# Attention scores of both query tiles of a head issued together, every second step, in a two-layer hybrid encoder

## What is computed

```python
# differential attention: 8 heads, two maps per head (m = 0, 1), head width 64, queries in blocks of 128
logits = jnp.einsum("bqhmd,bkhmd->bhmqk", q_blk, k) * scale
p = jax.nn.softmax(logits + bias[None, :, None], axis=-1)
attn = p[:, :, 0] - lam * p[:, :, 1]
out = jnp.einsum("bhqk,bkhe->bqhe", attn, v)
# beside it, independent of it: a bidirectional Mamba-2 scan (32 heads in 4 groups, 2 chunks of 128 tokens)
lmat = jnp.exp(segsum(a));  cb = C @ B.T;  y_diag = (cb * lmat) @ X;  y_off = C @ state * exp(a_cum)
```

## Time and profile before

| | us |
|---|---|
| device time, median of three runs | 1744.72 |
| lowest and highest of the three | 1743.62, 1745.13 |
| span of the profiled execution, first to last instruction | 1742.8 |
| PE busy | 1694.6 (97% of the span) |
| DVE, ACT, POOL busy | 713.3, 685.1, 668.0 |
| span of the attention and scan loop, each layer (from 198 to 303 in layer 0) | about 105 |

### The profile page before, as it was taken

One profiled execution on the slowest core, in us unless ns is written; L12 is line 12 of the kernel. 1 busy time (PEld: TensorE's weight loads), 2 busy tenths in 40 slices (PEclk: granted clock), 3 DMA queues, 4 the chain that ended last, 5 costly groups with the idle time before them and its releaser, 6 DMA issues.

```text
span 1742.8 us, 23270 instructions
## 1 busy us (share of the span) xinstructions
PE 1694.6 (97%) x8975; PEld 1056.7 (61%) x8975; DVE 713.3 (41%) x1345; ACT 685.1 (39%) x1549; POOL 668.0 (38%) x536
## 2 busy tenths in 40 slices
PE   8999999999999999899999999999999999999997
PEld 6889877787434444343378898777864344443343
DVE  5728788524212212121276387865241212222122
ACT  5565787754211111111156567877541111111111
POOL 7888876894000000000077887768930000000000
PEclk9999999999999999999999999999999999999999
DMA  7554312667999999999954442227589999999997
GB/s 271 195 193 152 140 49 108 274 259 308 363 415 427 428 427 428 427 428 428 411 229 165 179 189 97 97 80 300 219 333 398 420 427 427 428 427 428 428 425 303
DMA packets 50707, 528.47 MB, mean 303 GB/s; under 512 B 5496, under 2 KB 8312, under 8 KB 20128
## 3 DMA queue, kind: packets, MB, share of 16 engines
q1 hardware_dynamic: 50560, 526.89, 74.2%
q0 software_dynamic: 32, 0.02, 0.0%
HBM read 525.82 MB, written 1.06 MB: 302 GB/s over the span
## 4 chain that ended last, share of the span: by engine, by line
PE 68%; DMA 9%; DVE 9%; SPq 5%; ACT 5%; issue 2%; POOL 1%; DVEq 0%; ACTq 0%
PE PS L1297 19%; PE PS L1325 10%; DMA view<-in_w_exp_down_dram 9%; PE PS L875 8%; PE PS L877 8%; PE PS L876 8%; SPq L678 5%; DVE view L2003 5%; PE PS L1237 2%; PE PS L1223 1%; DVE view L1999 1%; PE PS L1082 1%; PE PS L1224 1%; PE PS L863 1%; ACT view L1571 1%
## 5 line engine op out<-in xcount | busy, mean ns | idle before, releaser
L2370 POOL TENSOR_TENSOR view<-view,view 128x512 fp32r<-128x512 f32 x448 | 579.8, 1315 | 548.1 <-ACT view L1457 537.3
L1297 PE MATMUL PS<-view,view 128*64 128x512 f32 x2044 | 457.8, 600 | 15.1 <-issue 14.5
L1457 ACT ACTIVATE view<-view 128x512 fp32r<-128x512 f32 x448 | 275.1, 633 | 149.1 <-PE PS L877 146.9
L1297 PEld LDWEIGHTS PS<-view,view 128*64 128x64 f32 x2044 | 150.9, 138 | 292.0 <-issue 288.7
L875 PE MATMUL PS<-view,view 128*128 128x512 f32 x704 | 286.0, 406 | 5.6 <-POOL view L2370 3.7
L877 PE MATMUL PS<-view,view 128*128 128x512 f32 x704 | 275.5, 391 | 0.0
L876 PE MATMUL PS<-view,view 128*128 128x512 f32 x704 | 275.4, 391 | 0.0
L1325 PE MATMUL PS<-view,stb 128*64 128x512 f32 x1024 | 230.4, 597 | 8.4 <-DMA view<-in_w_exp_down_dram 5.5
L2270 DVE SCALAR_TENSOR_TENSOR view<-PS,gcol,view 128x512 fp32r<-128x512 f32 x64 | 48.1, 751 | 448.7 <-ACT view L1770 448.6
L875 PEld LDWEIGHTS PS<-view,view 128*128 128x128 f32 x704 | 132.8, 189 | 33.5 <-issue 5.8
L1325 PEld LDWEIGHTS PS<-view,stb 128*64 128x64 f32 x1024 | 71.3, 136 | 132.6 <-issue 117.0
(11 more groups left out here) (260 smaller groups left out, 2024.0 us busy)
## 6 DMA issues: line engine op xcount, KB each, us to landing
view<-in_w_exp_up_dram SPq DMA_DIRECT2D x56, 2048.0 KB, 25.8
view<-in_w_exp_down_dram SPq DMA_DIRECT2D x56, 2048.0 KB, 28.1
view<-in_w_mix_dram SPq DMA_DIRECT2D x54, 2048.0 KB, 7.7
view<-in_w_exp_gate_dram SPq DMA_DIRECT2D x52, 2048.0 KB, 28.8
view<-in_w_exp_gate_dram SPq DMA_DIRECT2D x20, 512.0 KB, 31.2
view<-in_w_exp_down_dram SPq DMA_DIRECT2D x20, 512.0 KB, 14.9
view<-in_w_exp_gate_dram SPq DMA_DIRECT2D x8, 1024.0 KB, 8.1
view<-in_w_exp_up_dram SPq DMA_DIRECT2D x8, 1024.0 KB, 9.3
```

The source lines that it names most:

```text
L1297: ins = pe.matmul(bank(ph, name, j)[e * CAP:(e + 1) * CAP, :], xgT1[:, k, at + e * CAP:at + (e + 1) * CAP], rows, start=(k == 0), stop=(k ...
L1457: nc.scalar.activation(highs(chunk), weights(slot8, chunk), ACT.Copy).then_inc(*high_ready.up(ph))
L2370: g_.tensor_tensor(weights(low8, chunk), weights(slot8, chunk), highs(chunk), ALU.subtract).then_inc(*low_ready.up(ph))
```

## The change

`scores` is called once for each head, in the even step, and issues the products of both query tiles: those of the second tile go to columns 256 to 511 of the same two banks. There is one fill and one drain of the pair of banks for each head, where there were two. DVE reads columns 0 to 255 in the even step and 256 to 511 in the odd step; the even step's read counts on DVE's own step semaphore, and the odd step's read counts the drain. The number of matmuls, of DVE instructions and of bytes is the same.

```diff
@@ mixer_fills
-            f += [(("D", j, q), 4), (("sc", i), 6)]
+            f += [(("D", j, q), 4)] + ([(("sc", j), 6)] if q == 0 else [])
@@ SP
-                        sp.wait_ge(*out_of(ph, "sc", ATT - 1))
+                        sp.wait_ge(*out_of(ph, "sc", HEADS - 1))
@@ PE
-                def scores(i):
-                    h, qt = i // 2, i % 2
-                    pe.wait_ge(*free(ph, "sc", i))
-                    if i == 0:
+                def scores(h):
+                    pe.wait_ge(*free(ph, "sc", h))
+                    if h == 0:
                         pe.wait_ge(*out_of(ph, "xT", XT))
-                    for m in range(2):
-                        rows = slice(m * HD, (m + 1) * HD)
-                        ins = pe.matmul(PS[:, 6 + m, 0:TT * P], qT[rows, h, qt * P:(qt + 1) * P], kT[rows, h, :],
-                                        start=True, stop=True)
-                    ins.then_inc(*fill(ph, "sc", i))
+                    for qt in range(TT):
+                        for m in range(2):
+                            rows = slice(m * HD, (m + 1) * HD)
+                            ins = pe.matmul(PS[:, 6 + m, qt * TT * P:(qt + 1) * TT * P], qT[rows, h, qt * P:(qt + 1) * P],
+                                            kT[rows, h, :], start=True, stop=True)
+                    ins.then_inc(*fill(ph, "sc", h))
@@ PE, step i
                             decay_sums(i)
-                            scores(i)
+                            if q == 0:
+                                scores(j)
@@ DVE, step i
-                        dve.wait_ge(*full(ph, "sc", i))
+                        dve.wait_ge(*full(ph, "sc", h))
...
-                        v.scalar_tensor_tensor(out=lg[:, i % 2], in0=PS[:, 6:8, 0:TT * P],
-                                               scalar=HD ** -0.5, in1=bias, op0=ALU.mult, op1=ALU.add
-                                               ).then_inc(*drain(ph, "sc", i))
-                        dve.wait_ge(*out_of(ph, "sc", i))
+                        ins = v.scalar_tensor_tensor(out=lg[:, i % 2], in0=PS[:, 6:8, qt * TT * P:(qt + 1) * TT * P],
+                                                     scalar=HD ** -0.5, in1=bias, op0=ALU.mult, op1=ALU.add)
+                        if qt:
+                            ins.then_inc(*drain(ph, "sc", h))
+                            dve.wait_ge(*out_of(ph, "sc", h))
+                        else:
+                            link(ins)
```

More of the change, by code:

```diff
@@ L483, in encoder @@
         columns_in = sig("columns_in", 1, 0, step=16)
-        dve_step = sig("dve_step", 279, 0)
+        dve_step = sig("dve_step", 287, 0)
         sumsq = sig("sumsq", 2 * 4 + 8 + 1 + 2, 0)
```

## The result

Over nine executions each, the changed kernel takes 1748.19 us (1746.57 to 1751.33) where the kernel before takes 1744.18 us (1742.40 to 1745.40): a ratio of 1.002, 95% interval 1.0011 to 1.0028, or 4.0 us, of which the interval leaves 1.9 to 4.9. It lies in the forecast's range of 1741.2 to 1748.7, but above the part of it that was called likeliest (1744.5 to 1748.0), and is slower by about the smallest difference that can be told. The profiled execution took 1750.18 us itself, its span is 1748.2 us, 5.4 more than the span of before; another profiled execution of the same kernel (experiment 1) has a span of 1745.6, with a mean granted clock of 0.997 where this one has 0.994, so a single span is no measure here.

What follows compares the result with a forecast made beforehand. PE was taken to bound the loop, with DVE not far behind. Each layer shifts 5a - 2r = +0.63 us, +1.26 for two; 1744.7 + 1.3 gives 1746.0 us, range 1741.2 to 1748.7.

Steps and rivals of the forecast that it cites:

- Step 1: `off` keeps its 0.41 us wait for ACT; removing the scores only lengthens the wait, so PE's shift is 0.
- D(3) +0.43: Decay sums of step 3 stand behind the doubled scores and come 0.43 us later; exponentials and DVE's add follow.
- `aT(4)` in step 5 +0.43: Transposes in step 5 need DVE's map, already 0.27 us late, so step 5 starts 0.43 us later.
- D(7): Decay sums of step 7: step 5's +0.43 us plus one more a; after the odd step's saving, +0.10.
- a: PE time the second tile's scores add in an even step: 0.43 us taken, upper bound 0.63.
- r: PE time freed in each odd step by removing its scores: 0.76 us.
- The rival with the second tile in a row: Second tile's score products don't run side by side, a = 0.86: +5.6 us, 1750.3; chance 0.13.
- The signs: Rows to check: `aT` in steps 5 and 13 waits about 0.9 us, `y(7)` about 1.2, starting near 298.7.
- first rival: PE's saving comes through as steps 5 and 13 open up: 1741.6, or 1740.1 us; chance 0.20.
- the term - r between step 7 and step 11: PE saves r per odd step with inputs early: step 9 at -0.23 us, D(11) at +0.20.
- DVE's waits were not the bound: Rival: DVE's waits for scores bound the kernel, so 12.7 us go, giving 1732.0; chance 0.03.
- L2026 stretched beside POOL: In the first rival: DVE's L2026 takes 1.35 and 1.46 us beside POOL's products, 0.48 in step 9; unstretching one frees step 5.

Runs made afterwards that it cites:

- 2 `o` late, even: Changed kernel with the values product `o` moved behind D, and its copy on ACT behind the exponentials, in even steps: 1751.33 us, ratio 1.0040 to the kernel before.
- 4 scores in odd step: Changed kernel with both tiles' scores issued in the odd step before, behind the transposes `aT`: 1748.79 us, ratio 1.0023 to the kernel before.
- 12 copy early: Changed kernel with ACT copying the transposed map between fourth and fifth exponential in steps 7 and 9: 1748.93 us, ratio 1.0025 to the kernel before.
- experiment 5: Changed kernel with scores split in even steps, first tile's ahead of D, second tile's behind: 1752.02 us, ratio 1.0038 to the kernel before.
- experiment 9: Changed kernel with one weight piece moved from step 2 to 4 and one from 13 to 12: 1747.40 us, ratio 1.0016 to the kernel before.

## Why it came out so

**What held.** The whole line of the forecast up to step 7, and the wait that takes the place of DVE's:

- Step 1: a shift of 0 was forecast. `off` now waits 0.80 us for ACT instead of 0.41; what PE saved there became waiting.
- D(3) +0.43: 11.37 - 10.97 = +0.40. The rows of ACT and DVE behind it, against the earlier trace rows:

```profile
218.50 1.14 ACT L1598 ACTIVATE view<-PS,view 128x128 f32<-128x128 f32 x4 [0.53 <-PE PS L1013]
219.52 1.13 ACT L1598 ACTIVATE PS<-PS,view 128x128 f32<-128x128 f32 x4
220.52 0.43 ACT L1611 ACTIVATE view<-PS 128x256 f32<-128x256 f32 x1
```

```profile
220.69 0.69 DVE L2054 TENSOR_TENSOR view<-PS,view 128x512 f32<-128x512 f32 x1 [1.99 <-ACT PS L1598]
```

  DVE's wait at this add was 0.60 for the scores and 0.20 for ACT in step 3; it is 1.99 for ACT alone. D was what held it. (Part of the 1.99 is that DVE is earlier by a shorter map of step 2, see the rivals.)
- `aT(4)` in step 5 +0.43: 231.39 - 206.20 = 25.19 against 24.78 before, +0.41.
- D(7), which is that shift and one a more, +0.86: measured +0.87.
- a = 0.43 and r = 0.76: measured 0.43 and 0.73. The rival with the second tile in a row (a = 0.86) is out.
- The signs: `aT` in steps 5 and 13 shows waits of 0.62 and 0.89 us where about 0.9 was forecast, `y(7)` 0.85 where 1.2 was. `y(7)` starts at 297.52 and not near 298.7, which in the letter is a sign of the first rival ("before 298"). It is none: the loop as a whole starts 1.99 us earlier in this execution (206.20 against 208.19), as D(0) does ahead of any changed instruction, and only 0.36 us earlier in the second one.

**What failed: the term - r between step 7 and step 11.** The forecast gave PE r - a = 0.33 us in each of the heads between the two late maps ("step 9: +3a - 2r = -0.23"), because PE's inputs were early there. They were early by less than r. The shift of D(11) is +1.02 and not +0.20, that of `aT(12)` in step 13 is 75.76 - 74.73 = +1.03, and from there D(15) is at +1.48 and `y(7)` at +1.47, where +0.63 was forecast.

What the runs showed in its place is a limit on the time from the last group of D in an odd step to the first instruction of D in the even step behind it. Steps 3 and 4 of four kernels, and steps 7 and 8 of the last:

| kernel | D's last group, next D | us | what ends it |
|---|---|---|---|
| before | 219.60, 223.56 | 3.96 | PE's own work |
| changed | 218.02, 221.62 | 3.60 | ACT's copy, then `o` |
| 2 `o` late, even | 218.32, 221.73 | 3.41 | DVE's add frees bank 5 |
| 4 scores in odd step | 218.13, 222.58 | 4.45 | PE's own work |
| 12 copy early | 243.75, 247.48 | 3.73 | DVE's add, behind the copy |

The change takes the scores, 0.73 us, out of exactly this stretch. PE alone would need 3.96 - 0.73 = 3.23 us. ACT's exponentials and copy, with `o` behind them, allow 3.60; the exponentials and DVE's add allow 3.41. So an odd step gives 3.96 - 3.60 = 0.36 us, not 0.76. Put 0.36 for r in steps 7 and 9, and the forecast's own sum gives, from D(7) at +0.86: D(9) 0.86 - 0.36 + 0.43 = +0.93 (measured +0.96), D(11) +1.00 (measured +1.02), D(15) and `y(7)` +1.43 (measured +1.48 and +1.47). The term was mis-sized by 2 x 0.40 us a layer, 1.6 us in all, and with it the forecast's 1746.0 becomes 1747.6.

That the range held is in part luck. It had been drawn up to a = 0.63, and a is 0.43; the room meant for that was filled by a wait that the forecast did not have. It also helped that the median of before is 0.5 us lower in this comparison (1744.18) than where the forecast started (1744.72): the shift itself, 4.0 us, is above the largest that it named, 3.3.

Experiment 12 shows that both limits are there: with the one taken away in two steps, the other takes over at once. Nothing is won there because the edit also lengthens the other, from 3.41 to 3.73. Taking away the copy alone, without that push, could have won 3.60 - 3.41 = 0.19 us in such a step (an estimate from these rows; no run has it). Experiment 4 shows the same from the other side: with the double scores inside the stretch no limit is reached, and PE gains 0.21 us a head up to D(11).

Two readings of mine led past it. The kernel's description leaves steps 7 and 9 among those of which most have two pieces of weight product. They have one (before, six rows of it from 246.90 to 248.13), as ten of the 16 steps have: 0, 1, 3, 4, 7, 9, 11, 12, 14 and 15. Only the odd steps 5 and 13 have two, and there `aT` is late anyway. And I checked the slack of DVE's map in step 9 (2.5 us), but not that of the copy in step 8, nor that of bank 5. In the trace of before no bracket shows either, since PE was 0.36 and 0.55 us behind them.

The waits add up to the loop. PE's work fell by 7 x 0.30 = 2.1 us. `o` in five steps takes back 5 x 0.37 (0.73 - 0.36), 1.85 us; `aT` in step 5 comes 1.72 us after `off` where it took 1.23, 0.49; in step 13 1.96 against 1.23, 0.73; and `y(7)` in step 16 comes 1.52 us after `o` where it took 298.04 - 296.95 = 1.09, 0.43. That is 3.50 - 2.1 = 1.40 of the 1.47 us.

**Why a group is cheaper.** A group of the first tile alone costs 0.73 us, its second tile 0.43, and the two apart cost 0.3 us a head more (experiment 5). The Trainium skill, TensorEngine Tiling (Array Packing), section Key Properties, says that changing the tiling mode drains TensorE. Experiment 5 agrees, as it enters and leaves the 64-row products twice a head where the changed kernel does once. The page gives no figure for it, and no run here tells the change of mode from any other fixed cost that a group may have.

**The other rivals.** PE's saving did not come through, DVE's waits were not the bound. "L2026 stretched beside POOL" stayed as it was where it counts: 1.35 and 1.46 us in steps 4 and 5, in the changed kernel too, so moving DVE by 0.4 us did not move it off POOL's products. It did go away elsewhere: the map of step 2, made in step 3, took 1.31 us (it began at 218.75, POOL's product L2394 at 218.74) and takes 0.48 now (216.89, and POOL's at 217.16). That map stands ahead of DVE's wait for the exponentials, so the 0.83 us only lengthen the wait. That DVE's part of the chain is the reason that steps 5 and 13 are late is argued from the unbroken run of its rows; experiment 9 bears it out in part, as with D(3) and D(11) earlier against steps 5 and 13 the waits in both are gone. No experiment shortened DVE's run itself.

## What to carry to other kernels

Before taking work out of one engine's program, look at what stands on both sides of it: if the engine comes back to the same bank or buffer behind it, the removed work was covering the way through the other engines, and the gain ends where that way's length begins. Measure that length from release to return, from the rows, since a trace shows no wait where there are only a few tenths of slack; and where two such ways run side by side, compare both, as removing the longer one wins at most the difference between them (here 0.19 us), and less if the edit lengthens the other. Grouping calls saves their fixed cost, but the group is in front of something, and if that something starts the longest chain, what it costs there is paid at once, while what it saves elsewhere may be waited away.

## What was unexpected of the hardware

- A wait's bracket is shorter than its cost. The bracket on `o` in step 4 is 0.16 us and the step is 0.33 us late; in step 5 before, a matmul that came 0.27 us late had none; in step 13 now, one of 0.89 stands where `aT` is 1.96 - 0.96 = 1.00 us late. These brackets are 0.1 to 0.3 us short, and the ends of matmuls, from which they count, are modelled; the starts should be compared.
- Two 64-row fp32 products of 256 columns, each on one half of the array's rows, hold PE for 0.64 us, and four for 1.06 us (step 2 of experiment 5 and of the changed kernel). So the first two cost 0.64 us and the next two 0.42.
- A loop of 91 us repeats to 0.06 us between two executions of the changed kernel, while whole executions of 1745 us spread over 3 to 8 us. For a change of a few tenths the rows of one profile were the better instrument.
